# Context norm's transposes, squares and sums beside the expert output's norm, norm factors in the recurrence stage

## The reference, cut to what matters

```python
def rmsnorm(x, g):                       # first block
    r = rsqrt(mean(x * x, axis=-1) + EPS)
    return x * r * g

h = h + g2 * rmsnorm(ff, ffn_post_g)     # ff: output of the experts; end of the first block
...
h  = modulate(rms_norm(x,  norm1), shift1, scale1)                   # x is h from above, (512, 1024)
hc = modulate(rms_norm(xc, norm1), cc_mod[:D], cc_mod[D:2 * D])      # xc is the input ctx_2, (256, 1024)
u  = h @ w_in                            # and columns of w_in applied to hc as well
```

## Time and profile before

| | us |
|---|---|
| median of 3 runs | 3785.39 |
| lowest and highest of them | 3784.65, 3787.49 |
| the profiled execution | 3785.36 |
| its span, first to last instruction | 3783.5 |
| PE busy with matmuls | 3310.6 (88% of the span) |
| DVE busy | 1276.8 (34%) |
| ACT busy | 496.9 (13%) |

### The profile page before, as it was taken

One profiled execution on the slowest core, in us unless ns is written; L12 is line 12 of the kernel. 1 busy time (PEld: TensorE's weight loads), 2 busy tenths in 40 slices (PEclk: granted clock), 3 DMA queues, 4 the chain that ended last, 5 costly groups with the idle time before them and its releaser, 6 DMA issues.

```text
span 3783.5 us, 28754 instructions
## 1 busy us (share of the span) xinstructions
PE 3310.6 (88%) x11091; PEld 1625.8 (43%) x11092; DVE 1276.8 (34%) x2053; ACT 496.9 (13%) x853; POOL 252.1 (7%) x279
## 2 busy tenths in 40 slices
PE   4894758799999999999994797887868999899998
PEld 2352223544444444444441555535636444344444
DVE  2127982422322323223233338804334110222101
ACT  1211002200000010000100211112214100100000
POOL 0005540100000000000000001200000000000000
PEclk8986779699999999999997797897779999999999
DMA  9412411389899898998984010011010122212210
GB/s 291 167 67 75 145 45 31 128 320 339 312 340 339 321 341 311 340 339 321 341 313 166 23 45 12 1 39 34 1 45 1 56 78 73 72 67 78 71 63 22
DMA packets 288045, 583.67 MB, mean 154 GB/s; under 512 B 7953, under 2 KB 12492, under 8 KB 287884
## 3 DMA queue, kind: packets, MB, share of 16 engines
q1 hardware_dynamic: 281184, 561.20, 41.3%
q0 software_dynamic: 5456, 17.38, 1.9%
q10 hardware_dynamic: 1276, 3.29, 0.2%
HBM read 577.65 MB, written 4.19 MB: 154 GB/s over the span
## 4 chain that ended last, share of the span: by engine, by line
PE 77%; DVE 14%; ACT 3%; issue 2%; SPq 1%; POOL 1%; ACTq 1%; DMA 1%; DVEq 0%; POOLq 0%; PEldq 0%
PE psum_all L206 74%; DVE scratch L1190 4%; PE psum_all L214 3%; SPq L183 1%; DVE scratch L1214 1%; DVE scratch L2562 1%; DVE scratch L2975 1%; ACTq L559 1%; DVE scratch L2593 1%; DVE scratch L1207 1%; ACT scratch L3037 1%; DVE scratch L2590 1%; DMA panel<-in_ada_w 1%; DVE scratch L2856 0%; ACT hidden L417 0%
## 5 line engine op out<-in xcount | busy, mean ns | idle before, releaser
L206 PE MATMUL psum_all<-panel,scratch 128*64 128x512 f32 (+3 forms) x3264 | 1100.5, 595 | 1.6 <-ACTq L1771 0.8
L206 PE MATMUL psum_all<-hidden,panel 128*128 128x512 f32 (+1 forms) x1808 | 794.0, 601 | 31.2 <-ACT hidden L417 20.9
L206 PEld LDWEIGHTS psum_all<-panel,scratch 128*128 128x128 f32 (+1 forms) x3264 | 400.9, 165 | 523.0 <-issue 517.7
L206 PEld LDWEIGHTS psum_all<-hidden,panel 128*128 128x128 f32 (+1 forms) x1808 | 346.3, 192 | 470.1 <-issue 439.7
L206 PE MATMUL psum_all<-scratch 128*128 128x64 f32 (+7 forms) x1592 | 392.7, 443 | 147.1 <-DVEq L1228 82.4
L206 PEld LDWEIGHTS psum_all<-scratch 128*128 128x128 f32 (+1 forms) x1592 | 252.2, 241 | 256.6 <-issue 98.4
L1946 DVE TENSOR_TENSOR hidden<-hidden,psum_all 128x512 f32<-128x512 f32 x264 | 169.6, 684 | 282.7 <-PE psum_all L206 282.7
L214 PE MATMUL psum_all<-const,scratch 128*128 128x128 f32 (+3 forms) x977 | 156.4, 300 | 112.3 <-DMA scratch<-in_s_lambda_im 33.4
L206 PE MATMUL psum_all<-scratch,panel 128*128 128x512 f32 (+1 forms) x672 | 250.5, 531 | 2.0 <-DVE resid L3162 1.0
L214 PEld LDWEIGHTS psum_all<-const,scratch 128*128 128x128 f32 (+3 forms) x977 | 115.3, 156 | 208.8 <-issue 102.1
L206 PE MATMUL psum_all<-scratch,const 128*128 128x512 f32 (+4 forms) x212 | 107.7, 664 | 95.4 <-ACT scratch L408 44.8
(11 more groups left out here) (309 smaller groups left out, 2313.6 us busy)
## 6 DMA issues: line engine op xcount, KB each, us to landing
panel<-in_exp_w_gu SPq DMA_DIRECT2D x132, 2048.0 KB, 10.7
panel<-in_exp_w_down SPq DMA_DIRECT2D x66, 2048.0 KB, 10.8
panel<-in_w_in SPq DMA_DIRECT2D x17, 2048.0 KB, 8.2
panel<-in_ada_w SPq DMA_DIRECT2D x12, 2048.0 KB, 20.3
panel<-in_w_mod SPq DMA_DIRECT2D x12, 2048.0 KB, 7.8
panel<-in_ffn_w_gate SPq DMA_DIRECT2D x5, 2048.0 KB, 7.8
panel<-in_ffn_w_up SPq DMA_DIRECT2D x5, 2048.0 KB, 7.8
panel<-in_w_out SPq DMA_DIRECT2D x4, 2048.0 KB, 8.0
```

The lines of the kernel that those rows point to most:

```text
L206: ins = self.pe.matmul(out, lhsT, rhs, start=start, stop=stop)
```

## The change

In `dve_s5` the three norm factors are made right behind the bias on `mods2` (new function `dve_second_factors`). The transposed context goes to ACT's banks instead of DVE's. ACT reads each bank twice, once as a copy to `ctx_t` and once squared to `c_sq`, and signals `sq_ready` when both reads are done. Then it squares the tiles of `resid` as they come from DVE. Only then do the two roots follow, each with its shifts: first the context's, then `resid`'s. `resid_ready` is no longer raised or waited for here. `ctx_t` and `c_std` move to the end of `scratch`, and `c_sq` shares the room of `hc`, the context's normed form.

```diff
@@ dve_s5
             dve_mod_bias(dve, step, mods2, col("b_mod_2"), 2)
+            dve_second_factors(dve, step)
             dve.wait_ge(s5_gate.sem, s5_gate.next(dve))
@@ buffers
-        ctx_t = part(4096, DT, CTX)
-        c_sq, c_std = part(6144, DT, CTX), part(8192, CTX)
         x_sq, x_std = part(8704, DT, T), part(12800, T)
+        ctx_t, c_std = part(13312, DT, CTX), part(15360, CTX)
+        c_sq = hc
@@ pe_second_norms
-                pe.wait_ge(to_dve.free, to_dve.room())
-                bank = to_dve.fill()
+                pe.wait_ge(to_act.free, to_act.room())
+                bank = to_act.fill()
@@ DVE
-        def dve_second_norms(dve, step):
-            for m in range(DT):
-                dve.wait_ge(to_dve.full, to_dve.next_full())
-                bank = to_dve.take()
-                dve.tensor_copy(ctx_t[:, m, :], bank[:, 0:CTX]).then_inc(to_dve.free, 1)
-            dve.wait_ge(to_dve.free, to_dve.own_reads())
+        def dve_second_factors(dve, step):
             for factor, gain, m, which in (...):
...
-            dve.sem_inc(resid_ready.sem, 1)
+
+        def dve_second_norms(dve, step):
             dve_norm(dve, step, ctx_t, hc, c_std, DT, A1C)
             dve_norm(dve, step, resid, hidden, x_std, DT, A1X)
@@ act_second_norms
-            act.wait_ge(resid_ready.sem, resid_ready.next(act, 3))
-            act_norm(act, step, ctx_t, c_sq, c_std, ...)
-            act_norm(act, step, resid[:, :, :], x_sq, x_std, ..., after=resid_tile)
+            for m in range(DT):
+                act.wait_ge(to_act.full, to_act.next_full())
+                bank = to_act.take()
+                act.activation(ctx_t[:, m, :], bank[:, 0:CTX], ACT.Copy)
+                act.activation(c_sq[:, m, :], bank[:, 0:CTX], ACT.Square).then_inc(to_act.free, 1)
+                act.wait_ge(to_act.free, to_act.own_reads())
+                act.sem_inc(sq_ready.sem, 1)
+            for k in range(DT):
+                act.wait_ge(resid_tile.sem, resid_tile.next(act))
+                act.activation(x_sq[:, k, :], resid[:, k, :], ACT.Square).then_inc(sq_ready.sem, 1)
+            for src, std, n, which in ((hc, c_std, CTX, 1), (hidden, x_std, T, 0)):
+                act.wait_ge(to_act.full, to_act.next_full())
+                bank = to_act.take()
+                act.activation(std, bank[:, 0:n], ACT.Sqrt, ...).then_inc(to_act.free, 1)
+                act.wait_ge(to_act.free, to_act.own_reads())
+                act.sem_inc(std_ready.sem, 1)
+                for k in range(DT):
+                    act.wait_ge(scaled.sem, scaled.next(act))
+                    act.activation(src[:, k, :], src[:, k, :], ACT.Identity, bias=...).then_inc(normed.sem, 1)
```

More of the change, by code:

```diff
@@ L2251, in pe_second_norms @@
                     if t == CT - 1:
-                        ins.then_inc(to_dve.full, 1)
+                        ins.then_inc(to_act.full, 1)
             pe_norm(pe, mm, c_sq, CTX, DT)
             pe_norm(pe, mm, x_sq, T, DT)
-        def dve_second_norms(dve, step):
-            for m in range(DT):
-                dve.wait_ge(to_dve.full, to_dve.next_full())
-                bank = to_dve.take()
-                dve.tensor_copy(ctx_t[:, m, :], bank[:, 0:CTX]).then_inc(to_dve.free, 1)
-            dve.wait_ge(to_dve.free, to_dve.own_reads())
+        def dve_second_factors(dve, step):
             for factor, gain, m, which in ((A1X, "norm1_2", 8, 0), (A1C, "norm1_2", 8, 1), (A2X, "norm2_2", 32, 0)):
@@ L2270, in act_second_norms @@
         def act_second_norms(act, step):
-            act.wait_ge(resid_ready.sem, resid_ready.next(act, 3))
-            act_norm(act, step, ctx_t, c_sq, c_std, CTX, DT, D, [mods2[:, k, 1:2] for k in range(DT)], hc)
-            act_norm(act, step, resid[:, :, :], x_sq, x_std, T, DT, D, [mods2[:, k, 0:1] for k in range(DT)], hidden,
-                     after=resid_tile)
+            for m in range(DT):
[11 more added lines that the diff above has]
+                bank = to_act.take()
+                act.activation(std, bank[:, 0:n], ACT.Sqrt, scale=1.0 / D, bias=eps_col[:, 0:1]).then_inc(to_act.free, 1)
+                act.wait_ge(to_act.free, to_act.own_reads())
+                act.sem_inc(std_ready.sem, 1)
+                for k in range(DT):
+                    act.wait_ge(scaled.sem, scaled.next(act))
+                    act.activation(src[:, k, :], src[:, k, :], ACT.Identity, bias=mods2[:, k, which:which + 1])\
+                        .then_inc(normed.sem, 1)
         NC, NH = TT + CT, SSM_HEADS
```

## The result

The changed kernel takes 3761.05 us (median of 6 runs, 3759.1 to 3763.09) against 3784.88 us (6 runs, 3782.91 to 3787.49) for the kernel before in the same comparison: a ratio of 0.9937, 95% interval 0.9924 to 0.9950. Its profiled execution took 3759.1 us, with a span of 3757.3.

What follows compares the result with a forecast made beforehand. The prediction took the kernel as bound by TensorE (77% of the chain), idle through 36.9 us of serial steps before `pe_dt`. Terms: 9.4 + 10.5 = 19.9 us; 3785.4 - 19.9 = 3765.5 us, range 3761.5 to 3770.

Steps and rivals of the forecast that it cites:

- The stretch: From the start of the experts' squares to the start of `pe_dt`: said to get 19.9 us shorter.
- two terms, 9.4 and 10.5: Context's root 9.4 us earlier; 10.5 us of `resid`'s squares and sums gone ahead of the second root.
- The bank exchange: ScalarE's copy and square of each context bank, beside VectorE's adds: 0.8 us a bank (0.69 to 0.92).
- The limit of the cover: ScalarE's moved context work is hidden if it ends by 2077.5; each us beyond that costs one.
- Two ends in the prediction: TensorE's context sums, from about 2071, end at 2076.5 as before or 2078.2 at 1.2 GHz; hidden.
- TensorE's clock in the stretch: TensorE stands still from about 2084 to 2098, so `pe_dt` starts at half clock as before and takes 20.5 us.
- Rival C: Clock stays at 2.4 GHz until 2098, so `pe_dt` takes 10.3 us less; time 3752 us, chance 0.02.
- Rival A: TensorE's sums of `resid` end late at low clock, 4.1 us behind ScalarE; 3765.6 to 3769.6 us, chance 0.05.
- The factors: Three VectorE operations of 0.57 us, moved into the recurrence stage, hidden by a 14.56 us wait for ScalarE: cost 0.
- The range: Whole kernel: 3761.5 to 3770 us, allowing 1.2 us for the clock's rise, 2.8 for runs, 4.1 for late sums.
- How the numbers follow: Prediction's passage on time and chances: 3765.5 us at 0.88; faster 0.97, within 0.2% 0.02, slower 0.01.
- the five slices: Slices of the profile behind this place that show less than the full clock, cited for scatter of later rises.

Runs made afterwards that it cites:

- the early context alone: Changed kernel with the squares of `resid` put back behind the context's shifts: 3772.73 us, ratio 0.9964 to the kernel before.
- the order alone: Kernel before with ScalarE squaring `resid` ahead of the context's root, copies and factors left in place: 3775.37 us, ratio 0.9975.
- the padded pairs: Changed kernel with four more ScalarE copies of each context bank between its copy and its square: 3769.57 us, ratio 0.9960 to the kernel before.

## Why the prediction was right, and where it was wrong

**The stretch: right, step by step.** Counted from the start of the experts' squares, the forecast put the context's root at 29.35 us, the second root at 35.4, `pe_dt` at 45.8; they stand at 29.17, 35.22 and 45.55. The gain was to be 19.9 us and is 20.1. Its two terms, 9.4 and 10.5, stand in the changed kernel as 9.6 and 10.5. Run apart the halves gave 10.4 and 9.7, since the early context alone spares 1.0 us of last square and root, and the order alone pays 0.8 us for squares and sums in a row: the terms hold for the whole change and not for a half of it. The bank exchange was put at 0.8 us (0.69 to 0.92) and takes 0.78. The limit of the cover was confirmed with the padded pairs. Two ends in the prediction are off by a little: from 2071, sums of 5.70 and 6.8 us end at 2076.7 and 2077.8, not at 2076.5 and 2078.2; nothing hangs on it, since both sums ended at 2080.75, 4.5 us ahead of the second root.

**TensorE's clock in the stretch: right.** `pe_dt` starts at half clock and its 96 records take 20.5 us as before (2095.60 to 2116.10). Rival C is out. Rival A is out as well, and more clearly than forecast: the clock didn't fall between the transposes and the sums, so that the context's sums ran at 2.4 GHz. The rule of the Trainium skill, "TensorE: Matmul & The Clock Gate", Part 4: PE-mode transpose, that transposes don't count as work for the clock, was not put to the test in the changed kernel: they kept TensorE only from 2064.02 to 2068.5, and in the kernel before the clock held for as long without any work (from 2067.54 to about 2072.4). With the padded pairs the clock did fall among transposes, but there TensorE stood still for 1.45 us between them, so that run doesn't decide it either.

**The factors: right.** They are in the shadow of the gate's wait (13.96 us of it are left).

**The range: wrong.** The step that failed is in "How the numbers follow": the part behind `pe_dt` was held to move along unchanged, worth 0 in the sum, and its scatter was given 2.8 us from the spread of three runs and 1.2 us for one rise. Its length was 3.8 us less in three profiles of the changed kernel, and 1656.0 to 1665.6 us in all fourteen profiles. The sum then is 20.1 + 3.8 = 23.9 us, against 23.8, 24.4 and 23.9 measured. Of the 3.8 us, 3.1 are one fall of the clock in the second attention that doesn't come, 0.3 a shorter wait of ScalarE just ahead of it, and 0.4 smaller shifts before. Its scatter had been put too small as well: the 49 executions of the kernel before spread over 10.6 us. Profiles of one kernel don't show this, since they repeat it (1665.45 and 1665.55; 1661.70, 1661.59 and 1661.52); a delay or an edit does. Nor did the five slices that the prediction names point at it: the fall stands in the slice from 2838 to 2932, which reads 9. By how little the range was missed, 0.45 us, is luck: the median of the kernel before moved by 0.5 us itself, from 3785.39 to 3784.88, when three more runs were added.

The Trainium skill, "TensorE: Matmul & The Clock Gate", Part 1, says that the number of slow matmuls at a start varies between runs of one kernel, and that such a start costs under 1% of a typical span. That is about a start, and no run here takes one apart. What the runs show is the spread over all rises and falls behind `pe_dt` between kernels: 9.5 us of 1665, or 0.6%. It is small too, and yet nearly half of what this change brings.

## What to carry to other kernels

An engine that works in order should do what its inputs allow, not what belongs together: the squares of the second norm stood 16 us behind their inputs because they were written behind the first norm's shifts. Such a gain could be read off the trace here to 0.2 us as a whole, and to 1 us for a half of it, and the cover of the moved work gave the point from which it cost. What TensorE does 800 us later is not rigid, though: for a change of 0.5%, allow some 5 us either way (an estimate, half of the 9.5 us between the profiles here) for clock falls that come or go anywhere behind the edit, and compare stretches in the profiles beside the medians. A profile is one execution: see first where its time stands among the kernel's others.

## What the runs showed of the hardware that I had not expected

- A delay of 9.9 us ahead of `pe_dt` made the profiled span of the kernel before only 3.2 us longer (3786.7 against 3783.5), since TensorE needed 1480.33 us in place of 1486.91 for the same 4906 records behind it. The median rose by 6.7 us.
- One fall of the clock in the midst of the second attention costs 3.1 us. TensorE was busy for 66.9 of the 80 us ahead of it (5.6 of the last 8), and for 66.7 of the same 80 us in the changed kernel, where the clock didn't fall.
- A copy and a square of one PSUM bank on ScalarE start 0.28 us apart and take 0.38 us each, and with the wait for its own reads the pair comes every 0.78 us; VectorE's adds beside it took 0.69 us against 0.68 before.
